# Values of two attention groups by products that move 512 weight columns out of two slots of the split weights

## The reference, cut to what matters

```python
h = rmsnorm(x, g_mix_pre[l])
proj = h @ w_in[l]                      # 512 x 1024 by 1024 x 3080
fq, fk, fv = ...                        # first group: columns 0, 512 and 1024, 512 each
f_logit = proj[..., 1536:1544] + b_fgt[l]
cq, ck, cv = ...                        # second group: columns 1544, 2056 and 2568, 512 each
y_fox = forgetting_attention(fq, fk, fv, f_logit)
y_chk = chunked_relpos_attention(cq, ck, cv, rel_bias[l])
y = concatenate([rmsnorm(y_fox, g_fox_out[l]), rmsnorm(y_chk, g_chk_out[l])])
x = x + rmsnorm(y @ w_out[l], g_mix_post[l])
```

## Time and profile before

| | |
|---|---|
| time, median of 3 runs | 2127.82 us (2126.98 to 2131.33) |
| the profiled execution: time | 2125.25 us |
| the profiled execution: span on the core | 2123.5 us |
| mean granted TensorE clock | 0.997 |
| PE busy | 2074.6 us, 98% of the span |
| DVE, ACT, POOL busy | 1234.4, 830.5, 209.4 us |
| values of group 0 (`v0`) on PE | from 30.10 us |
| values of group 1 (`v1`) on PE, woven with attention | until 161.94 us |

### The profile page before, as it was taken

The page is one execution under the profiler, slowest core; times in us unless marked ns, Lnnn a source line. Parts: engine busy times, 40 slices in busy tenths (PEclk is TensorE's granted clock), DMA queues, the critical chain, the costliest instruction groups (busy, mean ns, idle before and its releaser), DMA issues.

```text
span 2123.5 us, 26469 instructions
## 1 busy us (share of the span) xinstructions
PE 2074.6 (98%) x10728; PEld 1644.8 (77%) x10728; DVE 1234.4 (58%) x1888; ACT 830.5 (39%) x1336; POOL 209.4 (10%) x176
## 2 busy tenths in 40 slices
PE   8999999999999999999999999999999999999998
PEld 7787977678878886666788888887777777888886
DVE  5566746446677777986534344465676755343442
ACT  5345544445323233225423223354464554232232
POOL 1321011011000004552000000100000010000001
PEclk9999999999999999999999999999999999999999
DMA  6313422016677762763232233121221232322321
GB/s 204 116 51 100 150 99 80 20 60 217 219 278 255 263 227 90 187 163 107 80 117 88 94 100 99 54 70 50 61 70 50 73 116 81 116 87 95 99 99 40
DMA packets 218554, 245.51 MB, mean 116 GB/s; under 512 B 9144, under 2 KB 203192, under 8 KB 212288
## 3 DMA queue, kind: packets, MB, share of 16 engines
q1 hardware_dynamic: 208784, 231.73, 33.1%
q10 hardware_dynamic: 9648, 12.08, 2.3%
HBM read 237.75 MB, written 3.78 MB: 114 GB/s over the span
## 4 chain that ended last, share of the span: by engine, by line
PE 90%; DVE 4%; ACT 3%; DMA 1%; issue 1%; SPq 0%; ACTq 0%; POOL 0%; DVEq 0%
PE bank L1330 25%; PE bank L1338 24%; PE bank L1334 24%; PE bank L1355 2%; PE bank L1359 2%; PE bank L1363 2%; PE bank L1467 1%; PE bank L1541 1%; PE bank L1518 1%; PE bank L1425 1%; PE bank L1410 1%; PE bank L1402 1%; DVE wL L1949 1%; PE bank L1450 1%; PE bank L1531 1%
## 5 line engine op out<-in xcount | busy, mean ns | idle before, releaser
L1330 PE MATMUL bank<-hH,wH 128*128 128x512 f32 (+1 forms) x1672 | 633.4, 396 | 17.5 <-ACT wH L1582 8.0
L1338 PE MATMUL bank<-hL,wH 128*128 128x512 f32 (+1 forms) x1672 | 616.9, 386 | 0.1
L1334 PE MATMUL bank<-hH,wL 128*128 128x512 f32 (+1 forms) x1672 | 616.3, 386 | 0.0
L1577 ACT ACTIVATE wH<-raw 128x1024 fp32r<-128x1024 f32 (+1 forms) x376 | 334.1, 938 | 362.0 <-PE bank L1338 291.1
L1949 DVE TENSOR_TENSOR wL<-raw,wH 128x1024 fp32r<-128x1024 f32 (+1 forms) x340 | 378.9, 1151 | 134.0 <-ACT wH L1577 133.9
L1330 PEld LDWEIGHTS bank<-hH,wH 128*128 128x128 f32 x1672 | 313.9, 188 | 107.9 <-issue 28.8
L1338 PEld LDWEIGHTS bank<-hL,wH 128*128 128x128 f32 x1672 | 314.2, 188 | 65.0 <-DVE hL L1969 0.9
L1334 PEld LDWEIGHTS bank<-hH,wL 128*128 128x128 f32 x1672 | 314.5, 188 | 63.7 <-issue 3.1
L1330 PE MATMUL bank<-hidH,wH 128*128 128x512 f32 x768 | 299.1, 389 | 1.9 <-ACT hidH L1740 1.9
L1338 PE MATMUL bank<-hidL,wH 128*128 128x512 f32 x768 | 298.9, 389 | 0.0
L1334 PE MATMUL bank<-hidH,wL 128*128 128x512 f32 x768 | 298.8, 389 | 0.0
(11 more groups left out here) (220 smaller groups left out, 2025.7 us busy)
## 6 DMA issues: line engine op xcount, KB each, us to landing
raw<-in_mlp SPq DMA_DIRECT2D x64, 1024.0 KB, 5.2
araw<-in_ada_w SPq DMA_DIRECT2D x48, 1024.0 KB, 5.1
raw<-in_w_ff SPq DMA_DIRECT2D x32, 1024.0 KB, 7.3
raw<-in_hgrn_in SPq DMA_DIRECT2D x32, 512.0 KB, 3.7
raw<-in_w_in SPq DMA_DIRECT2D x11, 1024.0 KB, 5.3
raw<-in_conv_in SPq DMA_DIRECT2D x16, 512.0 KB, 4.0
u<-conv_u ACTq DMA_DIRECT2D x24, 270.0 KB, 5.0
raw<-in_w_mv SPq DMA_DIRECT2D x4, 1024.0 KB, 5.1
```

The costliest lines, as they stand in the source:

```text
L1330: mm(out, wH[:, s, m:m + 128], xh[:, k, 0:width], start=k == 0, stop=False)
L1334: mm(out, wL[:, s, m:m + 128], xh[:, k, 0:width], start=False, stop=False)
L1338: i = mm(out, wH[:, s, m:m + 128], xl[:, k, 0:width], start=False, stop=k == KB - 1)
L1577: do(wH[:, s, c], raw[:, r, c], ACT.Copy).then_inc(*s_whi.up(n, x))
```

## The change

The two calls of `linear_tm` for `v0` and `v1` become calls of `wide_tm`. It takes one piece and appends the next one without a `take` of its own, and then makes, for each of four groups of 128 tokens, all eight blocks of rows with one product over the 512 columns of both pieces. The moving operand is read from two slots of `wH` or `wL` by an access pattern with a step between two runs of 256 (`v0`: slots 2 and 0, `v1`: slots 0 and 1). Each product waits for both pieces. The low splits that are due are emitted one half at a time, in the second, third and fourth token group. One eviction of 128 by 512 takes the place of two of 128 by 256. Per group of values 192 products become 96 and 8 evictions 4.

```diff
+    def wide_tm(self, tag, name, k0, c0, ncols, src, ev, width=T):
+        for c in range(0, ncols, 512):
+            n = self.take(name, k0, c0 + c, 256)
+            self.pieces.append((name, k0, c0 + c + 256, 256))
+            for i in range(width // 128):
+                b, after = self.lin.get()
+                part = dict(i=i, b=b, after=after, key=("lin", tag, c, i))
+                for k in range(0, KB, 2):
+                    self.do("lin_wide", n=n, src=src, part=part, ks=(k, k + 1))
+                    if k == 2 and i:
+                        self.lows(1)
+                    if k + 2 == KB:
+                        if i == width // 128 - 1:
+                            self.piece_done[n] = self.piece_done[n + 1] = part["key"]
+                        self.lin.put(b, *ev(tag, i, c, b, part["key"]))
+                    yield 1.0
...
-        run(self.linear_tm("v0", "w_in", 0, 1024, 512, src, to_v(0)))
+        run(self.wide_tm("v0", "w_in", 0, 1024, 512, src, to_v(0)))
...
-            yield from self.linear_tm("v1", "w_in", 0, 2568, 512, src, to_v(1))
+            yield from self.wide_tm("v1", "w_in", 0, 2568, 512, src, to_v(1))
...
+                elif kind == "lin_wide":
+                    n, src, p = it["n"], it["src"], it["part"]
+                    xh, xl = operand(src)
+                    out, x = banks[p["b"]][:], slice(128 * p["i"], 128 * p["i"] + 128)
+                    s, step = n % NSPLIT, 2048 * ((n + 1) % NSPLIT - n % NSPLIT)
+                    for k in it["ks"]:
+                        wh, wl = (view(w, 2048 * s + 256 * k, [[step, 2], [1, 256]]) for w in (wH, wL))
...
+                        for m in (n, n + 1):
+                            pe.wait_ge(*s_whi.at(m, quarter(m, k)))
+                        mm(out, xh[:, k, x], wh, start=k == 0, stop=False)
+                        for m in (n, n + 1):
+                            pe.wait_ge(*low(m).at(m, quarter(m, k)))
+                        mm(out, xh[:, k, x], wl, start=False, stop=False)
+                        pe.wait_ge(*s_lo.at(*src[1:], k))
+                        i = mm(out, xl[:, k, x], wh, start=False, stop=k == KB - 1)
...
-                    do(vt[:, g, i, c:c + 256], banks[it["b"]][:, 0:256], ACT.Copy, scale=small[:, 224 + i:225 + i]).then_inc(
-                        *s_act.up("v", g, i, c))
+                    do(vt[:, g, i, :], banks[it["b"]][:], ACT.Copy, scale=small[:, 224 + i:225 + i]).then_inc(
+                        *s_act.up("v", g, i))
```

More of the change, by code:

```diff
@@ L608, in ev @@
             def ev(t, i, c, b, key):
-                do("ev_v", lin=key, g=g, i=i, c=c, b=b)
-                return (("act", "v", g, i, c),)
+                do("ev_v", lin=key, g=g, i=i, b=b)
+                return (("act", "v", g, i),)
             return ev
@@ L1365, in tensor_program @@
                                 i.then_inc(*s_mm.up(*p["key"]))
+                elif kind == "lin_wide":
[5 more added lines that the diff above has]
+                        wh, wl = (view(w, 2048 * s + 256 * k, [[step, 2], [1, 256]]) for w in (wH, wL))
+                        if k == 0:
+                            for ev in p["after"]:
+                                pe.wait_ge(*event(ev))
+                        pe.wait_ge(*s_hi.at(*src[1:], k))
+                        for m in (n, n + 1):
[6 more added lines that the diff above has]
+                        i = mm(out, xl[:, k, x], wh, start=False, stop=k == KB - 1)
+                        if k == KB - 1:
+                            i.then_inc(*s_mm.up(*p["key"]))
                 elif kind == "close_rows":
@@ L1419, in tensor_program @@
                         for j in range(i + 1):
-                            pe.wait_ge(*s_act.at("v", g, j, 256 * (it["us"][0]["h"] // 4)))
+                            pe.wait_ge(*s_act.at("v", g, j))
                             for u in it["us"]:
@@ L1634, in scalar_program @@
                 elif kind == "ev_v":
-                    g, i, c = it["g"], it["i"], it["c"]
+                    g, i = it["g"], it["i"]
                     act.wait_ge(*s_mm.at(*it["lin"]))
                     act.wait_ge(*s_act.at("row_rstd", "mix"))
-                    do(vt[:, g, i, c:c + 256], banks[it["b"]][:, 0:256], ACT.Copy, scale=small[:, 224 + i:225 + i]).then_inc(
-                        *s_act.up("v", g, i, c))
+                    do(vt[:, g, i, :], banks[it["b"]][:], ACT.Copy, scale=small[:, 224 + i:225 + i]).then_inc(
+                        *s_act.up("v", g, i))
                 elif kind == "ev_gate":
```

## The result

| | before | after |
|---|---|---|
| median | 2128.49 us (21 runs, 2124.48 to 2132.66) | 2131.12 us (21 runs, 2129.17 to 2135.19) |
| ratio after to before | | 1.0014, 95% interval 1.0008 to 1.002 |
| profiled execution | 2125.25 us, span 2123.5 | 2132.88 us, span 2131.1 |

The ratio's interval lies above 1, so the kernel is a little slower, but by no more than the 0.2% that I named as the bound. The forecast was 2130.0, the range 2125.5 to 2132.5.

What follows compares the result with a forecast made beforehand. PE, busy for 98% of the span, was taken as the bound. Products -2.26, second pair +3.6 and clock +0.9 gave +2.2 us, 2127.5 for a profiled execution, 2130.0 with the median's 2.57 added; range 2125.5 to 2132.5.

Steps and rivals of the forecast that it cites:

- The products: PE in `v0` and `v1`: wide products in place of narrow pairs save 1.22 and 1.04 us, together 2.26 us.
- the bound of 4 ns a product: Reading two runs of 256 columns costs 0 to 4 ns a product, 0 to 0.8 us for 192; taken as 0.
- The evictions: In each group eight of 475 ns become four of 598 ns; ACT is off PE's path there, counted as nothing.
- The first pair: Splits of pieces 5 and 6 behind `v0`: late biases cost 0 at the first transposes, 1.2 us to spare.
- The second pair: Splits of pieces 12 and 13 at `v1`'s end delay the copy; PE waits 4.0 us before L1386, +3.6 us.
- The clock: Lowered clock behind PE's 4.0 us wait: 0 to 1.6 us lost on PE, about 0.9 us of it L1386's, passed on.
- the wait at 191 us: PE's wait of 0.84 us at 191.06, said to absorb the rest of the lowered clock's cost.
- The sum: -2.26 + 3.6 + 0.9 = +2.2 us: the profiled 2125.25 becomes 2127.5; by the median 2130.0.

Runs made afterwards that it cites:

- rows_first: Wide kernel with the gate_rows transfer issued ahead of the fetch that goes with piece 5's high split; 2132.28 us, ratio 1.0015 to before.
- order_alone: Kernel before, all products narrow, with only piece 12's high and low halves placed where the wide kernel has them; 2132.98 us, ratio 1.0019 to before.
- lows_behind: Wide kernel with the four low halves of pieces 12 and 13 placed behind the copy `heads` on DVE; 2126.69 us, ratio 0.9991 to before.
- highs_behind: Wide kernel with the high halves of pieces 12 and 13 placed behind the exponentials on ACT; 2126.0 us, ratio 0.999 to before.
- fill_wait: Wide kernel with four products nobody reads put on PE inside the wait before L1425; 2129.15 us, ratio 1.0006 to before.
- highs_again: The same kernel as `highs_behind`, measured a second time; 2126.19 us, ratio 0.9987 to before.
- v1_alone: Wide kernel with `v0` put back to narrow products, so only `v1` is wide; 2131.24 us, ratio 1.001 to before.
- low_half: Wide kernel with only piece 13's two low halves placed behind the copy `heads`; 2126.71 us, ratio 0.9994 to before.

## Why the prediction was right, point by point

- **The products.** Forecast -2.26 us. `v0` took 21.76 us instead of 21.81, and the first product behind `v1` starts 159.98 - 30.48 = 129.50 us after the first of `v0`, instead of 161.94 - 30.10 = 131.84: -2.34. Two runs of 256 columns are read as one of 512; the bound of 4 ns a product was not needed.
- **The evictions.** I took 598 ns for one of 512 columns from a row of another line, which copies without a scale; this one scales by the token's norm and takes 690. It stands in the chain in front of the high splits, but the chain of the forecast had only 0.5 us for it: splits at 160.4, measured, less 0.38, 160.39. So it is no part of an error there.
- **The first pair.** Cost 0 was right, the slack was not 1.2 us. Up to the biases the forecast holds: high splits at 52.6, `gate_rows` at 56.4, first bias at 64.7, measured, less 0.38, 52.64, 56.65 and 64.87. The divisions ended at 73.43 + 1.31 = 74.74, the transposes start at 74.81. I had missed that two low halves take 3.37 us and not 2.36 while POOL adds biases; the divisions took 1.31 us instead of 0.99. The kernel before shows it already, beside its own biases at 54.38:

```profile
54.86 3.17 DVE L1949 TENSOR_TENSOR wL<-raw,wH 128x1024 fp32r<-128x1024 f32 x2 [9.16 <-ACT wH L1577]
```

  That leaves the transposes 0.07 us. With the biases 1.7 us sooner, in `rows_first`, they start no sooner.
- **The second pair.** Forecast in distances of the first profile: exponentials 164.2, low splits 168.8, copy 173.4, last product 174.8 with 4.0 us of idle time. Measured, less 0.38: 164.18, 168.80, 173.34, 174.75 with 4.05. `order_alone` shows that the order makes the wait, `lows_behind` and `highs_behind` that it takes both bursts.
- **The clock.** This is the term that was mis-sized. I wrote 0.9 us for L1386, at most 1.6 in all, and let the wait at 191 us take the rest. In the first profile L1425 paid 0.94 and the rows behind it, up to the transposes behind piece 11, 1.5 more (1.66 to 4.10 in the table), 2.4 in all; the wait of the earlier trace rows took 0.91 of it. That wait is missing in the second profile of before, so it was no safe place to count on. Then the clock fell once more, from about 207.7 to 210.5 us, 1 us behind a wait of 1.07 us that both kernels have (203.24 us in before, 206.42 in after), and left another 0.7. In the second profile the first fall cost 1.7 instead of 2.4, and the second did not come. Over the five profiles with the wait the first fall cost 1.6 to 2.4 us. `fill_wait` gives 0.5 to 2.0 us for what is left at D2. So 0.9 is inside what was measured, at its lower end, and the bound of 1.6 was too low.
- **The sum.** Forecast +2.2, by medians +2.6; by position +3.5 and +2.0 against the first profile of before, +4.4 and +3.0 against the second. 0.7 of the 1.1 us between 2130.0 and 2131.12 is the base: 21 runs of before have 2128.49, the three that I had 2127.82. The two profiles of the wide kernel lost 3.75 and 4.8 us more behind 371 us than the first of before. The change touches no list there, and the medians leave no room for such a loss, but no run shows its cause.

## What to carry to other kernels

A wider product saved what the distances of the rows said, 2.3 us, and cost nothing by itself. What took it back was the list of another engine: work that had been spread over the stretch now came in one burst, in front of a chain on which PE waits. When a change joins two steps, write down which jobs of the other engines are released at the same moment now, and place each behind the operation that PE waits for next; here moving four instructions of ACT turned +2.6 us into -2.5 us by the medians. And price a wait of several us on PE at more than its length, by the half-speed rows behind it.

## What I had not expected of the hardware

- The same wait of 2.37 us at about 970 us is in all fourteen profiles. In the 4 us behind it the granted clock is 1.00 in five (both of before, `highs_behind`, `order_alone`, `fill_wait`) and 0.57 to 0.68 in the other nine, which costs about 1.6 us. `highs_behind` and `highs_again` are one kernel, and stand on either side. And 1 to 2 us behind the wait of 1.07 us, which ends between 201 and 207 us in all of them, the clock fell in five of the fourteen (after, `v1_alone`, `rows_first`, `low_half`, `lows_behind`). At 403 us waits of 1.65 and 0.56 us gave 0.61 in one profile of before and 1.00 in the other:

```profile
403.00:406.00 3.00, 2.42 (x6) 1.04 (x5) 0.11 (x1) 0.77 (x2) 0.00 (x0) 0.61 0.03 5
```

```profile
403.00:406.00 3.00, 2.54 (x6) 1.25 (x7) 0.00 (x0) 0.86 (x2) 0.00 (x0) 1.00 0.02 5
```

  Such falls are worth about as much as this change, and the 21 runs of a kernel are spread over 6 to 8 us.
- DVE's low split of half a piece takes 1.16 us alone (4.63 for four) and 1.69 us beside POOL's biases (3.37 for two).
- A wait of 1.77 us (`low_half`, one profile) left the clock at 1.00, one of 3.80 to 4.05 lowered it in all five profiles (of four kernels) that had it.
